# The low parts of fourteen weight units per layer computed by GpSimd instead of VectorE

## The reference

```
for l in range(2):
    h = rmsnorm(x)
    (q, k, v ... of four mixers) = split_columns(h @ w_in[l])
    y_nsa, y_swa, y_mla, y_fox = four mixers (8 heads each)
    merged = sum(sigmoid(h @ w_gate[l, i]) * (y_i @ w_branch[l, i]))
    x = x + rmsnorm(merged @ w_out[l])
    x = x + rmsnorm(memory_cross_attention(...))
    x = x + rmsnorm((silu(g) * u) @ ffn_w_out[l])
```

## Time and profile before

| | |
|---|---|
| median of 3 runs | 2817.48 us (2807.31, 2817.48, 2840.18) |
| span of the profiled execution | 2851.4 us |
| busy VectorE, ScalarE, GpSimd | 1574.1, 1165.3, 126.8 us |
| mean granted TensorE clock | 0.931 of full speed |

### The profile page before, as it was taken

How to read it: one execution, slowest core, us unless ns; L and a number is a source line. 1 busy time by engine, 2 the same in 40 slices (tenths; PEclk the granted TensorE clock), 3 DMA queues, 4 the chain that set the end, 5 groups by cost and what they waited for, 6 DMA issues and landing times.

```text
span 2851.4 us, 43271 instructions
## 1 busy us (share of the span) xinstructions
PE 2610.8 (92%) x13794; PEld 2142.9 (75%) x13794; DVE 1574.1 (55%) x3564; ACT 1165.3 (41%) x2432; POOL 126.8 (4%) x183
## 2 busy tenths in 40 slices
PE   1899899999999989999978998898999998999998
PEld 1776777778787878888867677786887886788886
DVE  3247886667375555553234478675755746455522
ACT  1225655464354442222222356463634545322222
POOL 3100000000001010000010000000000010100000
PEclk8779999999999889999987589998999998999999
DMA  4411112212313203333332110122132141133332
GB/s 78 113 42 46 31 39 67 56 56 67 81 53 119 67 23 91 95 101 89 94 92 57 30 38 28 49 67 59 46 82 74 59 126 38 48 95 100 94 94 70
DMA packets 343968, 196.39 MB, mean 69 GB/s; under 512 B 29340, under 2 KB 338704, under 8 KB 343152
## 3 DMA queue, kind: packets, MB, share of 16 engines
q1 hardware_dynamic: 340512, 178.02, 21.9%
q0 software_dynamic: 3280, 16.13, 2.5%
HBM read 186.78 MB, written 7.34 MB: 68 GB/s over the span
## 4 chain that ended last, share of the span: by engine, by line
PE 78%; DVE 9%; issue 5%; ACT 3%; DMA 2%; POOL 1%; DVEq 0%; ACTq 0%; POOLq 0%; SPq 0%
PE acc L1042 59%; PE o_acc L1042 4%; PE turn L1204 3%; PE scores L1042 2%; PE acc L1332 2%; PE scores L1095 2%; DVE ring L1614 1%; DMA w_f<-in_w_in_dram 1%; PE scores L1189 1%; ACT w_hi L727 1%; DVE q_tile L1593 1%; DVE p_lo L1554 1%; DVE w_lo L1457 1%; PE scores L1190 1%; PE o_acc L1117 1%
## 5 line engine op out<-in xcount | busy, mean ns | idle before, releaser
L1042 PE MATMUL acc<-h_hi,w_hi 128*128 128x512 f32 x1888 | 778.9, 413 | 38.9 <-DVE w_lo L1457 22.1
L1042 PE MATMUL acc<-h_lo,w_hi 128*128 128x512 f32 x1888 | 761.5, 403 | 0.0
L1042 PE MATMUL acc<-h_hi,w_lo 128*128 128x512 f32 x1888 | 761.3, 403 | 0.0
L1457 DVE TENSOR_TENSOR w_lo<-w_f,w_hi 128x1024 fp32r<-128x1024 f32 x336 | 411.4, 1224 | 572.5 <-ACT w_hi L727 570.6
L727 ACT ACTIVATE w_hi<-w_f 128x1024 fp32r<-128x1024 f32 x336 | 353.2, 1052 | 323.3 <-PE acc L1042 265.2
L1042 PEld LDWEIGHTS acc<-h_hi,w_hi 128*128 128x128 f32 x1888 | 369.9, 196 | 107.7 <-issue 21.7
L1042 PEld LDWEIGHTS acc<-h_hi,w_lo 128*128 128x128 f32 x1888 | 368.8, 195 | 78.9
L1042 PEld LDWEIGHTS acc<-h_lo,w_hi 128*128 128x128 f32 x1888 | 369.6, 196 | 64.7
L779 ACT ACTIVATE p_hi<-turn 128x256 fp32r<-128x256 f32 (+4 forms) x416 | 163.8, 394 | 339.1 <-PE turn L1204 338.2
L1554 DVE TENSOR_TENSOR p_lo<-turn,p_hi 128x256 fp32r<-128x256 f32 (+4 forms) x416 | 180.5, 434 | 103.8 <-ACT p_hi L779 101.8
L842 ACT ACTIVATE ring<-ring,neg_max 128x256 f32<-128x256 f32 (+4 forms) x416 | 208.5, 501 | 68.3 <-DVE neg_max L1614 67.2
(11 more groups left out here) (260 smaller groups left out, 3743.3 us busy)
## 6 DMA issues: line engine op xcount, KB each, us to landing
w_f<-in_ffn_w_in_dram SPq DMA_DIRECT2D x88, 512.0 KB, 3.8
w_f<-in_w_gate_dram SPq DMA_DIRECT2D x64, 512.0 KB, 3.8
w_f<-in_w_in_dram SPq DMA_DIRECT2D x62, 512.0 KB, 3.9
w_f<-in_w_branch_dram SPq DMA_DIRECT2D x32, 512.0 KB, 3.5
w_f<-in_ffn_w_out_dram SPq DMA_DIRECT2D x32, 512.0 KB, 3.8
w_f<-in_w_out_dram SPq DMA_DIRECT2D x16, 512.0 KB, 3.9
w_f<-in_ffn_w_out_dram SPq DMA_DIRECT2D x16, 384.0 KB, 3.3
x_spill<-trunk POOLq DMA_DIRECT2D x2, 2048.0 KB, 8.4
```

The costliest lines, as they stand in the source:

```text
L1042: ins = nc.tensor.matmul(dst, a, b, start=(n == 0 and not added), stop=(n == count - 1))
L1457: nc.vector.tensor_tensor(w_lo[:, u % 2, :], w_f32[:, u % 2, :], w_hi[:, u % 2, :].bitcast(F32), ALU.subtract).then_inc(w_ready, 1)
```

## The change

GpSimd gets its own `split_rest` and calls it fourteen times a layer, in its list behind the blocks of the compression weights. It waits for the low part of the unit before (so that `w_ready` still counts in order) and for the high part of this one. VectorE leaves out its fourteen. At the first unit of `br0` (the first that VectorE splits again) VectorE waits for GpSimd's last one.

```diff
+            def split_rest(l, u):
+
+                pool.wait_ge(w_ready, unit_at(l, u, 0) + 2)
+                pool.wait_ge(w_high, unit_at(l, u, 0) + 1)
+                pool.tensor_tensor(w_lo[:, u % 2, :], w_f32[:, u % 2, :], w_hi[:, u % 2, :].bitcast(F32),
+                                   ALU.subtract).then_inc(w_ready, 1)
+
             def power(l, name):
...
                 wait_apart(pool, blocks_zero, l * 4 + 4)
+                for ps in (CMP, SEL, WIN):
+                    for name, k in ps.filler:
+                        split_rest(l, UB[name] + k + 1)
                 power(l, "mlaq")
...
                     for n, (name, k) in enumerate(ps.filler):
-                        if ps.split_at(n) + 1 == s:
+                        if ps.split_at(n) + 1 == s and ps.gate is None:
                             next_unit(l, name, k, 0)
...
                 def body(k, j):
+                    if b == 0:
+                        dve.wait_ge(w_ready, unit_at(l, UB["br0"] + k + 1, j) + 2)
                     next_unit(l, f"br{b}", k, j)
```

## The result

| | kernel before | changed kernel |
|---|---|---|
| median of 17 runs each | 2827.74 us (2807.31 to 2878.23) | 2855.09 us (2826.51 to 2875.51) |
| profiled span, mean granted clock | 2851.4 us, 0.931 | 2867.4 us, 0.925 |
| VectorE busy in the span | 1574.1 us | 1580.9 us |
| GpSimd busy in the span | 126.8 us | 193.5 us |

A forecast was written before the change was run, and what follows sets the result against it. TensorE, busy 92% of the span, was taken as the bound. Starts -6.6, CMP of layer one +4.1, SEL and WIN +10.9 made +8.4 on 2817.5: 2825.9 us, own range 2812 to 2842, whole range 2800 to 2858.

The forecast's parts named there:

- The hold: Inside passes, GpSimd's low part and VectorE's divide exclude one another in SBUF; whoever comes second is held.
- GpSimd's duration: Each 128x1024 subtraction on GpSimd takes 2.4 us, between 2.25 and 2.6.
- The price of a held divide: Inside passes, each held divide costs 1.02 us in CMP of layer one, 0.78 in SEL and WIN.
- TensorE's waits for the divide: Sign in the profile after: in SEL and WIN they grow from 5.2 and 6.1 us to about 7.
- The starts: At the start of the six passes, VectorE's list loses one low part: gain 5 x 1.22 + 0.48 = 6.6 us.
- WIN's start in layer two: The one start where TensorE's wait is only 0.48 us, so the gain there is 0.48 us.
- The sum: Starts -6.6, CMP of layer one +4.1, SEL and WIN +10.9: +8.4 us in all.
- the second rival: The clock falls in CMP after new waits of about 1.2 us: 2852 us for one more pass, 2878 for two; 27%.
- in layer one the like gap of 1.37 us did nothing: Argument against the clock falling: TensorE's wait at CMP's start in layer one brought no fall.
- The clock is spared: Removing the wait at CMP's start saves up to 33.0 us where it made the clock fall: 2793 us; 4%.
- VectorE isn't held: Divides run beside GpSimd unheld; starts give 6.6 us and splits inside passes 6: 2805 us; 17%.
- would bring little: Inside passes, taking 1.2 us off VectorE alone gains little: the transpose waits only 0.20 us in CMP.

The follow-up runs named there:

- e3: Changed kernel with each of GpSimd's 28 low parts as four instructions on 128x256 instead of one on 128x1024; 2797.8 us, ratio 0.9881 to the kernel before.
- e8: Changed kernel with each of GpSimd's 28 low parts as two instructions on 128x512; 2802.6 us, ratio 0.9917 to the kernel before.
- e7: Kernel before, with GpSimd making only the 14 low parts inside SEL and WIN of both layers; 2850.5 us, ratio 1.0018.
- e1: Kernel before, with GpSimd making only the low part of each pass's first weight unit (6 of 28); 2817.0 us, ratio 0.9966.

## Why the prediction was right or wrong

**The hold: right in kind and in place.** That "whoever comes second is held, in both directions" was inferred from one row in which GpSimd was the loser. The trace after has the 22 divides that met GpSimd's low part in these passes all held to its end, and e3 and e8 dose the hold by GpSimd's instruction length alone.

**GpSimd's duration: right.** 2.4 us taken, 2.375 on the mean measured.

**The price of a held divide: too high by about 0.24 us.** This is the term that was mis-sized. The forecast let the divide start when GpSimd ends and then gave it its own 0.30 or 0.35 us. The held divide is over 0.04 to 0.09 us after GpSimd's end. So its end moves from 1.78 us after the high part to 2.54 in CMP, which is 0.76 and not 1.02, and from 2.07 to 2.61 in SEL and WIN, 0.54 and not 0.78. Where the clock was high, the transpose did follow 0.14 us behind it, as forecast, and waits 0.95 us in CMP, 0.22 to 0.37 in SEL and 0.74 to 0.81 in WIN. Measured by the intervals between `w_hi`, a held divide costs 0.8 us in CMP at the full clock, nothing at the low one (as expected for layer two), 0.1 to 0.8 in SEL and 0.5 to 0.6 in WIN. All 14 of SEL and WIN make about 7 us in e7's trace (7.6 by its level), where the forecast had 10.9. TensorE's waits for the divide stayed at 4.5 and 5.8 us instead of growing to 7.

**The starts: about right.** 6.6 expected. The first units of the passes are shorter by 1.2 (CMP), 0.3 to 1.1 (SEL) and 1.0 to 2.1 us (WIN), some 7 us in two layers, in the changed kernel. The level of e1, where the starts were changed alone, is only -3.0. WIN's start in layer two gains more than its 0.48: the scores waited for the queries there as well (2.30 us before, 0.37 after).

**The sum.** +8.4 expected at an unchanged clock. About 7 for SEL and WIN, less 7 for the starts, and 0 to +2 for what CMP has left at its lower clock make 0 to +2; the level measured +2.0 and +1.5.

**The clock: the second rival, not the forecast.** I gave it 27% against the forecast's 50%. Its picture was right: waits of 1 us inside CMP, and from the first of them on the pass runs at 0.50. That its 2852 us is so near the measured 2855 is partly luck: it stands on a median of three runs, 2817.5, while the median of 17 was 2827.7, and its path term of +8.4 was too high. What I had underrated is how often CMP falls without any change: I went by three runs and one profile, while 54 of 93 runs had fallen. That "in layer one the like gap of 1.37 us did nothing" was one case out of 14, and 8 of these 14 passes fell at that gap. The rival "The clock is spared" was right about this place, and missed that the new waits inside would bring the fall back. With 0.58 of the runs fallen before and 0.94 after, the mean clock cost moves by 0.37 x (402 - 363) = 14 us (the mean times at the lower level after and before), and the level adds 2. That makes +16, which is what the means of the 17 runs of the changed kernel and the 93 later runs of the kernel before differ by (2855.5 and 2839.5). The medians of the first comparison differ by 27, and how much of that was the draw of its 17 runs before can't be told.

**Not foreseen.** That relief and hold hide one another. The rival "VectorE isn't held" was priced at -12.6 us; e3 and e8, in which it is held for shorter pieces, measure -14 to -16 us and have no falls of the clock in 18 runs on top. The sum has no term for the relief inside a pass, which "would bring little"; taking the 7 us of the starts from -14 to -16 leaves 7 to 9 us that e3 and e8 gained inside.

## What to carry to other kernels

When work goes from VectorE to GpSimd, look for VectorE's next instruction that reads two SBUF tensors or scales one in SBUF, and cut GpSimd's work so that this one is let in early. Here two pieces instead of one turned +0.9% into -0.8%, though GpSimd worked longer; longer or shorter pieces than halves and quarters were not tried. Judge each step by two numbers, its time at equal granted clock and the share of runs in which the clock fell: a stage that is near a fall can make a neutral edit look like 0.7%. And before you reorder a list to get one instruction out early, look at what will stand behind the moved one.

## What the hardware showed beyond the expected

- A held VectorE instruction is recorded as busy: 0.30 us of work shows as 2.01. A busy share that rises after work was taken away is the sign of it.
- The hold ends with GpSimd's instruction, not with its list: between two pieces, with no gap between them in the trace, the divide got in (0.37 us beside quarters, 0.92 beside halves, 2.01 beside the whole). The divide after it then met the later pieces: 0.84 us beside quarters, 0.82 beside halves.
- A held divide is over 0.04 to 0.09 us after GpSimd's instruction ends, where its whole work takes 0.30 to 0.35 us unheld.
- GpSimd's subtraction took 733 ns for 128x256, 1284 for 128x512 and 2375 for 128x1024 on the mean, VectorE's waiting turns included: about 2.1 ns a column and 0.2 us fixed. The fixed part that the forecast had assumed is there.
- In CMP one and the same stretch of 258 matmuls took 47.5 or 77.3 us by the granted clock, in one and the same profiled execution. In the 14 profiled executions every fall in CMP came within 3 us behind a wait of TensorE of 0.5 to 1.4 us. What exactly tips it stays open, since many such waits have no fall behind them.
